# State-space decays: TensorE's broadcast against a broadcast by transfers, with VectorE's differences

## What is computed

```python
def step(state, inp):
    xc, dtc, bc, cc = inp
    cum = jnp.cumsum(dtc * A, axis=1)
    seg = cum[:, :, None] - cum[:, None, :]
    decay = jnp.exp(jnp.where(causal, seg, -jnp.inf))
    cb = jnp.einsum('btgn,bsgn->btsg', cc, bc)
    w = cb[..., None] * decay * dtc[:, None]
    y = jnp.einsum('btsgk,bsgkp->btgkp', w, xc)
    ...
```

## Time and profile before

| | us |
|---|---|
| median of 3 runs | 2634.89 (2634.13 to 2637.31) |
| span of the profiled execution | 2634.5 |
| PE busy | 2569.5 (98%) |
| DVE busy | 1362.8 (52%) |
| ACT busy | 1094.1 (42%) |
| POOL busy | 1169.8 (44%) |
| stretch of the eight groups | from about 1205 to 1621 in the span |

### The profile page before, as it was taken

The page is one execution under the profiler, slowest core; times in us unless marked ns, Lnnn a source line. Parts: engine busy times, 40 slices in busy tenths (PEclk is TensorE's granted clock), DMA queues, the critical chain, the costliest instruction groups (busy, mean ns, idle before and its releaser), DMA issues.

```text
span 2634.5 us, 32314 instructions
## 1 busy us (share of the span) xinstructions
PE 2569.5 (98%) x13086; PEld 2162.8 (82%) x13086; DVE 1362.8 (52%) x2097; ACT 1094.1 (42%) x1880; POOL 1169.8 (44%) x634
## 2 busy tenths in 40 slices
PE   7999999999999999999999999999999999999997
PEld 6888988888889888887777877888888888888886
DVE  6776540523435505337675675661653674651644
ACT  5554531334225413324563554542433554542432
POOL 3333663445455743452334333544445425544443
PEclk9999999999999999999999999899999999999999
DMA  5222333333333333323222222223323112323322
GB/s 156 60 71 60 95 96 97 96 96 86 99 96 89 96 97 98 99 62 86 67 73 80 73 67 69 73 81 112 98 86 95 38 56 73 84 80 117 96 84 68
DMA packets 436006, 224.26 MB, mean 85 GB/s; under 512 B 14865, under 2 KB 433937, under 8 KB 435857
## 3 DMA queue, kind: packets, MB, share of 16 engines
q1 hardware_dynamic: 435856, 222.18, 29.8%
HBM read 219.01 MB, written 2.10 MB: 84 GB/s over the span
## 4 chain that ended last, share of the span: by engine, by line
PE 91%; DVE 5%; ACT 2%; POOL 1%; issue 1%; DMA 0%; SPq 0%; DVEq 0%; POOLq 0%; ACTq 0%
PE ps L521 29%; PE ps L523 28%; PE ps L522 28%; PE ps L2661 1%; PE ps L2647 1%; PE ps L1507 1%; PE ps L1424 1%; POOL wl L495 0%; DVE acc L1486 0%; DVE acc L1480 0%; DMA xT<-in_xT 0%; PE ps L1530 0%; PE ps L2649 0%; ACT wh L487 0%; PE ps L2686 0%
## 5 line engine op out<-in xcount | busy, mean ns | idle before, releaser
L495 POOL TENSOR_TENSOR wl<-stg,wh 128x1024 fp32r<-128x1024 f32 (+4 forms) x447 | 1002.9, 2250 | 1227.8 <-ACT wh L487 1218.3
L521 PE MATMUL ps<-hh,wh 128*128 128x512 f32 (+2 forms) x2292 | 862.9, 376 | 29.4 <-DVE hl L1072 11.1
L523 PE MATMUL ps<-hh,wl 128*128 128x512 f32 (+2 forms) x2292 | 851.9, 372 | 0.0
L522 PE MATMUL ps<-hl,wh 128*128 128x512 f32 (+2 forms) x2292 | 851.3, 371 | 0.0
L487 ACT ACTIVATE wh<-stg 128x1024 fp32r<-128x1024 f32 (+4 forms) x447 | 436.1, 985 | 311.8 <-DMA stg<-in_mlp_w_down 110.4
L521 PEld LDWEIGHTS ps<-hh,wh 128*128 128x128 f32 (+1 forms) x2292 | 435.4, 190 | 107.2 <-issue 18.8
L521 PE MATMUL ps<-bh,wh 128*128 128x512 f32 (+1 forms) x1320 | 492.7, 373 | 6.0 <-POOL wl L495 4.4
L523 PEld LDWEIGHTS ps<-hh,wl 128*128 128x128 f32 (+1 forms) x2292 | 435.0, 190 | 74.6
L522 PEld LDWEIGHTS ps<-hl,wh 128*128 128x128 f32 (+1 forms) x2292 | 435.7, 190 | 71.6 <-issue 1.0
L523 PE MATMUL ps<-bh,wl 128*128 128x512 f32 (+1 forms) x1320 | 489.1, 371 | 0.0
L522 PE MATMUL ps<-bl,wh 128*128 128x512 f32 (+1 forms) x1320 | 488.9, 370 | 0.0
(11 more groups left out here) (320 smaller groups left out, 2664.8 us busy)
## 6 DMA issues: line engine op xcount, KB each, us to landing
stg<-in_ffn_up SPq DMA_DIRECT2D x88, 512.0 KB, 3.8
stg<-in_mlp_w_up SPq DMA_DIRECT2D x64, 512.0 KB, 4.0
stg<-in_mlp_w_down SPq DMA_DIRECT2D x64, 512.0 KB, 4.0
stg<-in_ssd_in_proj SPq DMA_DIRECT2D x48, 512.0 KB, 3.9
stg<-in_attn_w_qkv SPq DMA_DIRECT2D x24, 512.0 KB, 4.0
stg<-in_conv_w_in SPq DMA_DIRECT2D x24, 512.0 KB, 3.8
stg<-in_ffn_down SPq DMA_DIRECT2D x32, 384.0 KB, 3.3
stg<-in_ffn_down SPq DMA_DIRECT2D x32, 320.0 KB, 3.1
```

What stands on the lines that cost most here:

```text
L495: pool.tensor_tensor(wl[:, slab.slot, w], stg[:, slab.slot, w], wh[:, slab.slot, w].bitcast(F32), ALU.subtract).then_inc(s.lo_done, 1)
L521: pe.matmul(po, lh, rh, start=start, stop=False)
L522: pe.matmul(po, lh, rl, start=False, stop=False)
L523: return pe.matmul(po, ll, rh, start=False, stop=stop)
```

## The change

1. The running sums (32 heads, 1,280 columns each) are written to a buffer `running` in DRAM once (`store`), and SP waits for that.
2. For each head one transfer reads its row of 5,120 bytes 128 times, onto all partitions of a decay buffer (`spread_sums`): 640 KB a head, 32 transfers. There are four decay buffers in place of two. The transfers of a pair wait for the outputs of the same pair of the group before, on SP, between loads of slabs.
3. VectorE subtracts cum[s] and bounds the difference at zero, in place, in four instructions a head (`bound_sums`): the second pair of a group behind head 1's weights, the first pair of the next group behind head 3's weights.
4. ScalarE exponentiates a head in one instruction of 1,280 columns.
5. VectorE multiplies the four diagonal blocks of the C-B products, in PSUM, by a matrix of ones and zeros (`mask_cb`) before head 0's weights; the copy to `cb` is gone, and the weights read the products from PSUM.
6. TensorE's `decays` is gone, and so are the tables `CUM` and the steps that made them.

A semaphore of the latent attention (`kr_zero`) is merged with another; it counts the same events.

```diff
-        def decays(self, pe, i, k):
-
-            j = i + self.g0
-            if k == 0:
-                pe.wait_ge(s.cb_copied, 3 * j + 3)
-            else:
-                pe.wait_ge(s.e_done, 16 * j + 4 * k)
-            for r in (0, 1, 3, 2):
-                row, off = TRI[r]
+        def spread_sums(self, sp, j, pair):
+
+            for k in (2 * pair, 2 * pair + 1):
+                if j == 0 and k == HPG - 1:
+                    sp.wait_ge(s.cum_t, 3)
+                if j:
+                    sp.wait_ge(s.y_done, 2 * j - 1 + pair)
                 h = HPG * j + k
-                pe.matmul(ps[:, 3 + row, off:off + T - r * P], sel[:, h:h + 1].to_broadcast([P, P]),
-                          CUM[row][:, off:off + T - r * P], start=True, stop=False)
-                end = pe.matmul(ps[:, 3 + row, off:off + P], mask_r, ident_r, start=False, stop=True)
-                if r != 1:
-                    end.then_inc(s.decay_done, 1)
+                sp.dma_start(self.decay[k].rearrange("p a t -> p (a t)")[:, 0:RUN_W],
+                             running[h:h + 1, :].to_broadcast([P, RUN_W])).then_inc(s.decay_in[pair], 16)
...
         def head_exps(self, act, i, k):
+
             j = i + self.g0
-            for n, r in enumerate((0, 1, 3, 2)):
-                row, off = TRI[r]
-                act.wait_ge(s.decay_done, 12 * j + (SEED + 3 * k + (1, 2, 2, 3)[n]))
-                w = slice(off, off + T - r * P)
-                c = 4 * j + (r * SSD_H + k)
-                bias = neg_cum[:, c:c + 1] if isinstance(c, int) else stg[:, TABLES, bass.ds(c, 1)]
-                act.activation(self.decay[k % 2][:, row, w], ps[:, 3 + row, w], ACT.Exp, bias=bias).then_inc(s.e_done, 1)
+            act.wait_ge(s.e_arg, 4 * (HPG * j + k) + 4)
+            e = self.decay[k].rearrange("p a t -> p (a t)")[:, 0:RUN_W]
+            act.activation(e, e, ACT.Exp).then_inc(s.e_done, 1)
...
+        def mask_cb(self, dve, i):
+
+            j = i + self.g0
+            dve.wait_ge(s.cb_done, 3 * j + 3)
+            for r in range(TB):
+                row, off = TRI[r]
+                m = ps[:, 3 + row, off:off + P]
+                dve.tensor_tensor(m, m, causal, ALU.mult).then_inc(s.cb_masked, 1)
+
+        def bound_sums(self, dve, j, pair):
+
+            dve.wait_ge(s.decay_in[pair], 32 * (j + 1))
+            for k in (2 * pair, 2 * pair + 1):
+                for r in range(TB):
+                    row, off = TRI[r]
+                    c = HPG * j + r * SSD_H + k
+                    e = self.decay[k][:, row, off:off + T - r * P]
+                    dve.tensor_scalar(e, e, cum_nat[:, c:c + 1], 0.0, ALU.subtract, ALU.min).then_inc(s.e_arg, 1)
...
+                e = self.decay[k][:, row, off:off + T - r * P]
+                dve.scalar_tensor_tensor(e, e, dt_nat[:, c:c + 1], ps[:, 3 + row, off:off + T - r * P],
+                                         ALU.mult, ALU.mult).then_inc(s.w_done, 1)
...
+                        if k == 1:
+                            self.bound_sums(dve, i + self.g0, 1)
                         if k == 2:
                             self.skip_and_gate(dve, i, 0)
+                        if k == 3 and i + self.g0 + 1 < GROUPS:
+                            self.bound_sums(dve, i + self.g0 + 1, 0)
```

101 lines of the change are left out of this document (47 added, 54 removed).

## The result

The changed kernel takes 2669.2 us in the median of four runs (2665.4 to 2679.3), the kernel before 2636.1 beside it (2634.1 to 2641.7): a ratio of 1.0131, with a 95% interval of 1.0108 to 1.0153. The forecast was 2665, in a range of 2632 to 2690. The sign is right and the size is 4 us off, but, as will be seen, some of its terms missed and cancelled.

The account below looks back on a forecast made before the run. TensorE was taken as the bound by busy time, with the VectorE/ScalarE chain as long to 0.3 us; 32.5 + 0.8 + 1.2 - 0.7 - 3.5 = +30.3 on 2634.9 gave 2665, range 2632 to 2690.

Parts of the forecast that it names:

- rounds of groups 1, 2, 3, 5: Rounds with a group norm ahead: 52.8 us in place of 46.3, +6.5 each, both GpSimd collisions included.
- group 6, and group 7 to its last outputs: Group 6 +6.5 like other norm rounds; group 7, without projections ahead or `silu`, loses its decays: -0.7.
- groups 0 and 4: Groups without a group norm ahead, so without the first collision: +0.8 and +1.2.
- ahead of group 0, within the stage: Before group 0, the tables' copy on ScalarE and subtraction on VectorE are gone: -3.5.
- VectorE's chain: First taps to head 3's weights: 27.9 - 2.7 (weights) + 1.1 (mask) + 2.4 (bounds) + 0.4 (exponential) = 29.1 us.
- the exponential: ScalarE's one piece of 1,280 columns, 1.26 us: +0.4 on VectorE's chain for head 2, nothing for head 3.
- The first meeting: GpSimd's slab 1 subtraction comes amid VectorE's `y_low`; second half and `silu` wait, +2.6 in groups 1, 2, 3, 5, 6.
- The second meeting: Next group's bounds behind head 3's weights meet GpSimd, 2.4 more; slab 3's `silu` is late, `turn_x` starts 3.1 later.
- TensorE did not stay the bound: Rival at the outputs of heads 2 and 3: bounds slip into VectorE's waits, whole 34.5 gained, 2600; chance 0.12.
- The clock rival: Idle around the second outputs puts projection 5 at half speed: 2.6 in seven rounds, +18, 2683; chance 0.20.
- The late transfers: Rival: 640 KB transfers above 7 us each decide; at 12, 25 more in eight groups, near 2830; chance 0.05.
- The Trainium skill's figure: Bounds at 0.91 us a head instead of the row's 1.21, giving 2657; the forecast kept the row.

Follow-up runs that it names:

- run l: Run d with the masked C-B products copied by ScalarE into SBUF and read there by the weights; 2659.8 us.
- run a: Changed kernel with the four mask products moved ahead of the first taps; 2652.8 us.
- run c: Changed kernel with the bounds of heads 2 and 3 (second pair) moved ahead of the first taps; 2668.4 us.
- run m: Run d with the norm moved ahead too, plus head 2's exponential before the copy of the first outputs and the first group's second pair moved; 2606.4 us.
- second profile: Profile of the changed kernel measured once more, unaltered, to see its spread; median 2669.5 us.
- run o: Changed kernel with GpSimd held at both meeting places and 14 idle matmuls ahead of the second outputs; 2639.5 us.
- n: Changed kernel with GpSimd held back at both meeting places, nothing moved on VectorE; 2648.7 us.
- b: Changed kernel with the bounds of the next group's first pair moved behind the sum of the squares; 2651.4 us.
- run d: Changed kernel with mask and second pair's bounds ahead of the first taps, next group's first pair behind the sum of the squares; 2617.0 us.
- run f: Changed kernel with one added wait: GpSimd's slab behind the z gates is held until the next group's first-pair bounds are done; 2653.8 us.

## Why the prediction was right, point by point

The forecast's sum for the profiled execution, beside what the two traces give:

| term | forecast | measured |
|---|---|---|
| rounds of groups 1, 2, 3, 5 | 4 x 6.5 = 26.0 | 3.6 + 3.3 + 7.0 + 3.6 = 17.5 |
| group 6, and group 7 to its last outputs | 6.5 - 0.7 = 5.8 | 9.2 |
| groups 0 and 4 | 0.8 + 1.2 | 1.6 + 1.2 |
| ahead of group 0, within the stage | -3.5 | -4.6 |
| upstream of the stage | 0 | +5.6 |
| behind the last outputs | 0 | -1.3 |
| sum | 30.3 | 29.1 (of the unrounded terms) |

**VectorE's chain** was right to 0.15 us: 29.1 forecast, 28.95 measured where nothing met. Of its parts, the weights lost their 2.7 us of waiting, and run l shows that it was the place of the source (the forecast leaned on taps beside GpSimd's slab, which its rows do not show; the trace has that slab at 1320.50); the mask is worth 0.9 (run a) where 1.1 was counted; the second pair 2.4 (run c, in its undisturbed rounds); the exponential 0.3 to 0.5, of which run m got 0.36 a round back.

**The first meeting** is the step that was mis-sized. It costs 2.2 us where 2.6 was said, and it was taken to happen in all five rounds: two had it in one execution, four in another. What it also does was not forecast: it takes the wait away from the second outputs and leaves one of 2.4 to 2.5 us (once 4.5) at `turn_x`, behind which the clock fell in both rounds of the first profile (1.6 and 1.5 us) and in three of four of the second. The argument, "now GpSimd comes in its middle", rested on a few tenths of a us between the two engines, and took as certain what two rounds with the same 0.01 us between them settled differently.

**The second meeting** was right: in every round, 4.5 to 4.6 us for eight bounds (in group 3 of the second profile two of them met GpSimd, 6.64). `turn_x` started 2.7 us later than full-speed outputs would let it (5.0 - 2.3), where 3.1 was forecast. With both meetings a round took 51.8 us (forecast 52.8), and 53.5 where the clock fell behind `turn_x`, with the second alone 49.6 (50.2), with neither 47.5 (47.7, run o).

**The rounds' deficit was filled by terms that the forecast had not.** The clock on the path, 3.7 us in groups 1, 3, 5 and 6 together, is in the first two rows of the table; without it the missing first meetings would show more. The last group, 2.2 us longer where 0.7 less was forecast (group 6 is 7.0 of the 9.2): its `y_low` met GpSimd twice, in 1.98 and 2.87 us instead of 0.69 each, ahead of the outputs' own rounded slabs; nothing in the forecast spoke of a meeting there. The rows, VectorE and GpSimd:

```profile
1625.87 1.98 DVE L2970 TENSOR_TENSOR bl<-xT,bh 128x512 fp32r<-128x512 f32 x1
1627.77 2.87 DVE L2970 TENSOR_TENSOR bl<-tmp,bh 128x512 fp32r<-128x512 f32 x1
...
1624.88 5.21 POOL L499 TENSOR_TENSOR wl<-stg,wh 128x1024 fp32r<-128x1024 f32 x2 [4.77 <-ACT wh L491]
```

And 5.6 us come from upstream, from code that the change does not touch; the other profiles put that start on either side, so it is taken as chance of this execution, worth nothing in a median. By the profiles, then, the stage is 24.9 us longer; the medians differ by 33.1, and the second profile has 33.4 in the stage. The first profile is of the shortest of its four executions. The nearness of 2665 to 2669 owes something to luck; the rounds' structure does not.

**The rivals.** TensorE did not stay the bound in the changed kernel, but it would have, had the bounds lain in VectorE's waits, as the rival said: 2600 was its price, and run m reached 2606. The clock rival had the fall right, and the place in part. Mostly it fell over the second outputs, behind the longer delay of the SiLU, where it costs nothing until the meetings are away (9 us then, run o). But projection 5 did run at half clock where the rival had put it, in two of its seven rounds in the first profile, and with the ends in groups 1 and 5 that is 3.7 us of the profiled execution, not 18. The forecast had this at nothing. The late transfers fell: 4.2 to 5.6 us each, below the 7 from which they would count.

**The Trainium skill's figure** ("VectorE: DVE Perf Modes", section "The TRN2 errata") gave an estimate of 0.91 us a head for the bounds. Eight bounds in a row took 2.36 us, 1.18 a head, as the row of 1.21 had it; the measurement decides against the figure here.

So the 33 us of the medians split, by runs n and o, into 20.5 for the two meetings together with the clock at and behind `turn_x` (3.7 us in the first profile, 5.2 in the second; no run parts the two), 9.2 for the clock at the second outputs that the meetings hide, and 3.4 for VectorE's longer order, from which the shorter start is already taken. These are differences of runs that lift one layer after another; in another order the shares would differ, as runs a, b and c show.

## What to carry to other kernels

Work taken from the busiest engine paid here only where the engine that got it did it in its waits: the changed kernel's own instructions were 1.3% slower than the kernel before where they stood first, and 0.8% faster with three steps moved into VectorE's waits (run d). When two engines stand in each other's way as VectorE and GpSimd do here, look at every VectorE instruction whose tensors are all in SBUF and that lies within a few us of GpSimd's long ones: a meeting forecast from a few tenths of a us is a chance, not a fact, and a wait on the engine that has time (run f) can settle it. Delays come in layers, so take the uppermost away before you price the next one.

## What the runs showed of the hardware

- Which of VectorE and GpSimd starts first by the profile did not settle their meeting. With GpSimd ahead by 0.01 us both times, VectorE passed two instructions in one round and one in the next, and GpSimd's slab took 3.56 and 2.95 us in place of 2.4. VectorE's instructions with a PSUM source (taps, weights at 1.91 a set) ran through GpSimd's slabs unharmed, and a difference of 256 columns with an SBUF source took 2.44.
- The same meeting lies upstream: an instruction of four columns took 1.43 us beside a slab in the changed kernel's profile (124.12) and 0.19 in the other (119.52), and the stage's start lay anywhere within 8 us in the 14 profiles; that such meetings make this spread is likely, not shown. VectorE in the changed kernel, and GpSimd:

```profile
124.12 1.43 DVE L1757 TENSOR_SCALAR sm<-sm 128x4 f32<-128x4 f32 x1 [1.77 <-ACT tmp L1671]
...
123.14 2.38 POOL L499 TENSOR_TENSOR wl<-stg,wh 128x1024 fp32r<-128x1024 f32 x1 [6.18 <-ACT wh L491]
```

- Waits of 1.8 us ahead of the outputs left TensorE at full clock (0.65 us for 512 columns, at 1337.99). In the 14 profiles, from 1220 to 1655 us, the granted clock stayed at 1.00 behind 41 of 42 waits of 1.5 to 1.85 us. It fell to 0.50, for up to some 4 us, behind 28 of 30 waits of 2.8 to 3.2 us (not in a round of run a and group 4 of run f) and behind all 31 longer ones. Between these it went either way: a wait of 2.43 us at `turn_x` left 1.00 in group 2 of the second profile of the changed kernel and brought 0.50 in group 6 of the first. With 14 idle matmuls ahead of them (run o) the clock was 1.00 over the second outputs.
